# Hybrid SSD/S5 block on one core: the gate stage's x reaches token-major form by block transposes and transfers, and ScalarE applies dt

## The reference, cut to what matters

```
cb     = einsum("bclgn,bcsgn->bgcls", Cc, Bc)          # per group: tokens x tokens
decay  = exp(segsum(A))                                 # per head: tokens x tokens, lower triangle
y_diag = einsum("bgcls,bgrcls,bcsgrp->bclgrp", cb, decay, x * dt)
y      = (y_diag + d_skip * x) * silu(z), then an RMS norm over each group's 384 channels
```

## Time and profile before

| what | value |
|---|---|
| median of the runs | 1680.54 us (1680.04 to 1681.38) |
| the profiled execution's own time | 1680.3 us |
| its span, first to last instruction | 1678.6 us |
| PE busy | 1667.1 us (99%) |
| DVE busy | 1320.3 us (79%) |
| ACT busy | 962.7 us (57%) |
| POOL busy | 216.4 us (13%) |
| granted TensorE clock, mean | 0.998 of full |
| DMA, mean | 214 GB/s |

### The profile page before, as it was taken

One profiled execution on the slowest core, in us unless ns is written; L12 is line 12 of the kernel. 1 busy time (PEld: TensorE's weight loads), 2 busy tenths in 40 slices (PEclk: granted clock), 3 DMA queues, 4 the chain that ended last, 5 costly groups with the idle time before them and its releaser, 6 DMA issues.

```text
span 1678.6 us, 24422 instructions
## 1 busy us (share of the span) xinstructions
PE 1667.1 (99%) x8340; PEld 1395.1 (83%) x8340; DVE 1320.3 (79%) x1685; ACT 962.7 (57%) x1271; POOL 216.4 (13%) x310
## 2 busy tenths in 40 slices
PE   9999999999999999999999999999999999999997
PEld 8888888888788888888888888888888888888886
DVE  7999999999998986545775868888878888845555
ACT  7676676766666667444557755444444444454553
POOL 7843342221000000000000200000000000000001
PEclk9999999999999999999999999999999999999999
DMA  7666766666666566656786577777777777666653
GB/s 254 213 197 199 204 206 200 193 188 190 194 217 231 191 219 189 199 191 201 239 254 232 174 233 241 243 241 244 242 244 241 245 232 248 225 194 195 191 189 123
DMA packets 174569, 358.49 MB, mean 214 GB/s; under 512 B 16880, under 2 KB 39584, under 8 KB 174368
## 3 DMA queue, kind: packets, MB, share of 16 engines
q1 hardware_dynamic: 162528, 338.26, 62.5%
q0 software_dynamic: 11248, 18.37, 4.6%
q10 hardware_dynamic: 720, 0.93, 0.2%
HBM read 335.41 MB, written 15.80 MB: 209 GB/s over the span
## 4 chain that ended last, share of the span: by engine, by line
PE 73%; DVE 2%; issue 0%; ACT 0%; DVEq 0%
PE psum L1822 22%; PE psum L1823 22%; PE psum L1824 22%; PE psum L1783 3%; PE psum L1785 2%; PE psum L1908 1%; DVE wlo L1107 0%; PE psum L1909 0%; DVE vn L1749 0%; PE psum L1933 0%; DVE bc L1303 0%; PE psum L1829 0%; PE psum L1924 0%; DVE dec L1416 0%; PE psum L1982 0%; PE psum L1979 0%
## 5 line engine op out<-in xcount | busy, mean ns | idle before, releaser
L1107 DVE TENSOR_TENSOR wlo<-raw,whi 128x1024 fp32r<-128x1024 f32 x580 | 709.6, 1230 | 321.3 <-ACT whi L666 314.0
L666 ACT ACTIVATE whi<-raw 128x1024 fp32r<-128x1024 f32 x580 | 611.9, 1058 | 577.1 <-PE psum L1824 455.1
L1783 PE MATMUL psum<-act,whi 128*128 128x512 f32 x1088 | 342.5, 396 | 0.0
L1822 PE MATMUL psum<-whi,nw 128*128 128x512 f32 x704 | 274.1, 389 | 0.0
L1824 PE MATMUL psum<-whi,nw 128*128 128x512 f32 x704 | 273.9, 389 | 0.0
L1823 PE MATMUL psum<-wlo,nw 128*128 128x512 f32 x704 | 273.9, 389 | 0.0
L1785 PEld LDWEIGHTS psum<-act,wlo 128*128 128x128 f32 x1088 | 204.4, 188 | 48.3
L1785 PE MATMUL psum<-act,wlo 128*128 128x256 f32 x1088 | 213.7, 278 | 0.0
L1783 PEld LDWEIGHTS psum<-act,whi 128*128 128x128 f32 x1088 | 165.6, 189 | 3.3 <-issue 2.8
L1824 PEld LDWEIGHTS psum<-whi,nw 128*128 128x128 f32 x704 | 132.1, 188 | 27.6
L1822 PEld LDWEIGHTS psum<-whi,nw 128*128 128x128 f32 x704 | 132.1, 188 | 27.3
(11 more groups left out here) (251 smaller groups left out, 2300.3 us busy)
## 6 DMA issues: line engine op xcount, KB each, us to landing
raw<-in_w_up SPq DMA_DIRECT2D x176, 512.0 KB, 4.9
raw<-in_w_zx SPq DMA_DIRECT2D x96, 512.0 KB, 3.7
raw<-in_w_down SPq DMA_DIRECT2D x88, 512.0 KB, 3.8
raw<-in_w_gate SPq DMA_DIRECT2D x64, 512.0 KB, 5.6
raw<-in_w_proj SPq DMA_DIRECT2D x48, 512.0 KB, 4.4
raw<-in_w_bc SPq DMA_DIRECT2D x32, 512.0 KB, 3.7
raw<-in_w_glu SPq DMA_DIRECT2D x32, 512.0 KB, 4.4
raw<-in_w_out SPq DMA_DIRECT2D x32, 512.0 KB, 4.8
```

The lines of the kernel that those rows point to most:

```text
L666: fn(whi[:, s, :], raw[:, s, :], ACTF.Copy).then_inc(hi_ready, 1)
L1107: V.tensor_tensor(wlo[:, s, :], raw[:, s, :], whi[:, s, :], ALU.subtract).then_inc(lo_ready, 1)
L1783: mm(psum[:, b + t, :], whi[:, s, cols(t)], x, start=first, stop=False)
L1822: mm(banks[:, t, :], x_hi, high[:, k], start=j == 0 and k == 0, stop=False)
```

## The change

TensorE's six transposes a turn, ScalarE's copies to `bst` and `xst` and VectorE's two multiplications by dt go. In their place, for each group:

1. VectorE turns x in blocks of 32x32 (`x_turned`, two STREAM_TRANSPOSE instructions of 128x384): group 0's before the first bc turn, group 1's in turn 0 behind lo(4), group i+1's in turn i ahead of lo(2).
2. Four DMAs write the blocks to a scratch in DRAM (`token_write`, 96 KB each), and one DMA reads them back with tokens on the partitions into `xraw` (`token_fetch`, 384 KB). For group 0 SP issues these in the bc stage; for the others GpSimd does, around its decay loads.
3. ScalarE multiplies by dt (`tokens(g, k)`): 12 activations of 128x64 a turn, each with its own per-partition factor. They stand between hi(1) and decay(1), in turn 0 behind decay(1).

CB now reads B and C straight from `bc`; `heads(0)` waits for `xtok_ready` too. In turn 0 the transposes of dt move ahead of CB, and VectorE copies dt first.

The diff, cut to what the prediction speaks of:

```diff
@@ SP, bc stage @@
+                        if j == 6:
+                            first_tokens_write()
+                        if j == 24:
+                            first_tokens_fetch()
...
@@ GpSimd @@
-            with pool.Fori(0, GROUPS - 1) as i:
-                for half in range(2):
-                    pool.wait_ge(y_ready, i * 2 + (half + 1))
-                    load_decay(i + 1, half)
+            def token_write(g):
+
+                pool.wait_ge(x_blocks, g + 1)
+                for a in range(4):
+                    pool.dma_start(tokens_at[g % 2, :, :, a, :].rearrange("q j x -> j q x"),
+                                   xblk[g][32 * a:32 * a + 32, :, :, :, :].rearrange("j q k t i -> j q (k t i)")
+                                   ).then_inc(x_written, 16)
+
+            def token_fetch(g):
+
+                pool.wait_ge(x_written, 64 * g)
+                if g > 1:
+                    pool.wait_ge(xtok_ready, g)
+                pool.dma_start(xraw[g][:, :, :, :, :].rearrange("p a k t i -> p (a k t i)"),
+                               tokens_at[g % 2].rearrange("q j a x -> (q j) (a x)")).then_inc(x_read, 16)
+
+            for i in range(GROUPS - 1):
+                token_write(i + 1)
+                pool.wait_ge(y_ready, i * 2 + 1)
+                load_decay(i + 1, 0)
+                token_fetch(i + 1)
+                pool.wait_ge(y_ready, i * 2 + 2)
+                load_decay(i + 1, 1)
...
@@ ScalarE, gate_turn @@
-                def stage(g):
-                    fn(bst[:, :], bc[:, ds(g, 1), 0, :].rearrange("p o n -> p (o n)"), ACTF.Copy).then_inc(staged, 1)
-                    fn(xst[:, :, :], zx[:, ds(g * TPG, TPG), 1, :], ACTF.Copy).then_inc(staged, 1)
+                def tokens(g, k):
+
+                    act.wait_ge(x_read if g else first_read, 16 * max(g, 1))
+                    for hd in range(HPG):
+                        a = hd % 2 * 2
+                        ins = fn(xtok[:, k, 64 * hd:64 * hd + 64].rearrange("p (a i) -> p a i", a=2),
+                                 xraw[g][:, a:a + 2, k, hd // 2, :], ACTF.Identity,
+                                 scale=dtt[:, k, g * HPG + hd:g * HPG + hd + 1])
+                    if k == 1:
+                        ins.then_inc(xtok_ready, 1)
...
                     decay(1)
+                    act.wait_ge(dtt_ready, 1)
+                    tokens(0, 0)
+                    tokens(0, 1)
                 else:
                     hi(0)
                     decay(0)
                     hi(1)
+                    tokens(i, 0)
+                    tokens(i, 1)
                     decay(1)
...
-                if not last:
-                    act.wait_ge(cb_ready, i + 1)
-                    act.wait_ge(xp_ready, i + 1)
-                    stage(i + 1)
...
@@ VectorE @@
+            def x_turned(g):
...
+                for k in range(2):
+                    ins = V.transpose(xblk[g][:, :, k, :, :].rearrange("p q t i -> p t q i"),
+                                      zx[:, TPG * g:TPG * g + TPG, 1, k * P:k * P + P]
+                                      .rearrange("p t (q i) -> p t q i", q=4))
+                ins.then_inc(x_blocks, 1)
+
+            x_turned(0)
             mixer_turn("bc", 0, 6, ("zx", 5, 3))
...
-                    for k in range(2):
-                        ins = V.tensor_tensor(
-                            xtok[:, k, :].rearrange("p (h n) -> p h n", h=HPG),
-                            XP[k].rearrange("p (h n) -> p h n", h=HPG),
-                            dtt[:, k, ds(i * HPG, HPG)].rearrange("p (h o) -> p h o", o=1).to_broadcast([P, HPG, 64]),
-                            ALU.mult)
...
                     if not first_scan:
                         lo(1)
+                    if i < GROUPS - 1:
+                        x_turned(i + 1)
                     lo(2)
...
                 lo(4)
+                if prev is None:
+                    x_turned(1)
                 lo(5)
...
@@ TensorE, gate_turn @@
                     pe.wait_ge(m_ready, i * 2 + (half + 1))
+                    if half == 0:
+                        pe.wait_ge(xtok_ready, i + 1)
...
-                for k in range(2):
-                    for t in range(TPG):
-                        ins = nc.tensor.transpose(XP[k][:, t * P:t * P + P], xst[:, t, k * P:k * P + P], ident[:, :])
-                ins.then_inc(xp_ready, 1)
```

More of the change, by code:

```diff
@@ L164, in build_program @@
         dec = [at(f"dec{k}", [P, HALF, ML], F32, W + k * 4608) for k in range(2)]
-        xst = at("xst", [P, TPG, L], F32, W + 9216)
+        xblk = [at(f"xblk{g}", [P, 4, 2, TPG, 32], F32, off * K)
+                for g, off in enumerate((154, 140, 140, 140, 152, 152, 152, 152))]
+        xraw = [at(f"xraw{g}", [P, 4, 2, TPG, 32], F32, off)
+                for g, off in enumerate((147 * K, *[W + 9216] * (GROUPS - 1)))]
         xtok = at("xtok", [P, 2, HPG * 64], F32, W + 12288)
@@ L335, in up_fetch, with first_tokens_write, first_tokens_fetch @@
                              blocks_at.rearrange("j p q x -> (j p) (q x)")).then_inc(up_read, 16)
+            def first_tokens_write():
+                sp.wait_ge(x_blocks, 1)
+                for a in range(4):
+                    sp.dma_start(tokens_at[0, :, :, a, :].rearrange("q j x -> j q x"),
+                                 xblk[0][32 * a:32 * a + 32, :, :, :, :].rearrange("j q k t i -> j q (k t i)")
+                                 ).then_inc(first_written, 16)
+            def first_tokens_fetch():
+                sp.wait_ge(first_written, 64)
+                sp.wait_ge(cz_ready, 16)
+                sp.dma_start(xraw[0][:, :, :, :, :].rearrange("p a k t i -> p (a k t i)"),
+                             tokens_at[0].rearrange("q j a x -> (q j) (a x)")).then_inc(first_read, 16)
             for c in range(4):
@@ L353, in _ @@
                     sp.dma_start(craw[:, :, :, :], a["s5_c"]).then_inc(c_in, 16)
+                if name == "bc":
+                    for j in range(groups * quads):
+                        n = UNIT0[name] + j
+                        sp.wait_ge(lo_ready, n - RING + 1)
+                        sp.dma_start(raw[:, n % RING, :], a["w_bc"][j]).then_inc(w_in[n % RING], 16)
+                        if j == 6:
+                            first_tokens_write()
+                        if j == 24:
+                            first_tokens_fetch()
+                    continue
                 if name == "up":
@@ L770, in group_tap @@
                 act.nop(nofuse=True)
+                if name == "bc" and i == 0 and r == 1:
+                    act.wait_ge(first_written, 64)
                 for t in range(2):
@@ L864, in gate_turn @@
                     act.wait_ge(y5_ready, 8)
-                    act.wait_ge(xbc_done, 16)
-                    stage(0)
                     group_tap("bc", 1, 3)
@@ L898, in gate_turn @@
                 act.wait_ge(unit_used, u0 + 8)
+                if i == GROUPS - 2:
+                    act.wait_ge(x_written, 64 * (GROUPS - 1))
                 fn(gates[:, i, :, :], chunk_banks("gate", i), ACTF.Copy).then_inc(gate_free, 1)
@@ L1390, in _ @@
                 step.leave(6)
+            def x_turned(g):
+                if g == 0:
+                    dve.wait_ge(xbc_done, 2)
+                elif g == 1:
+                    dve.wait_ge(y5_ready, 8)
+                elif g == GROUPS - 1:
+                    dve.wait_ge(xbc_done, 12)
+                if g > 1:
+                    dve.wait_ge(x_written, 64 * (g - 1))
+                for k in range(2):
[4 more added lines that the diff above has]
+            x_turned(0)
             mixer_turn("bc", 0, 6, ("zx", 5, 3))
@@ L1424, in blocks, with mask_cb @@
                                     ALU.mult).then_inc(m_ready, 1)
-                def tokens():
+                def mask_cb():
                     dve.wait_ge(cb_ready, i + 1)
-                    V.tensor_tensor(cbm[:, :], CB, mask_in[:, :], ALU.mult)
-                    dve.wait_ge(xp_ready, i + 1)
                     if prev is None:
-                        step.done(V.tensor_copy(dtt[:, :, :], DTT))
-                    for k in range(2):
-                        ins = V.tensor_tensor(
-                            xtok[:, k, :].rearrange("p (h n) -> p h n", h=HPG),
-                            XP[k].rearrange("p (h n) -> p h n", h=HPG),
-                            dtt[:, k, ds(i * HPG, HPG)].rearrange("p (h o) -> p h o", o=1).to_broadcast([P, HPG, 64]),
-                            ALU.mult)
-                    step.done(ins)
+                        V.tensor_copy(dtt[:, :, :], DTT).then_inc(dtt_ready, 1)
+                    step.done(V.tensor_tensor(cbm[:, :], CB, mask_in[:, :], ALU.mult))
                 if prev is None:
@@ L1449, in gate_turn @@
                     lo(3)
-                    tokens()
+                    mask_cb()
                     blocks(0)
@@ L1921, in gate_turn @@
                     pe.wait_ge(y5_out, 8)
```

(8 more changed lines are left out.)

10 lines of the change are left out of this document (6 added, 4 removed).

## The result

The changed kernel takes 1683.03 us (median of 14 runs, 1681.72 to 1686.47), the kernel before 1680.53 (14 runs on the same chip, 1679.68 to 1681.65): a ratio of 1.0015, 95% interval 1.0008 to 1.0022. It is slower by 2.5 us, or 0.15%, where 1680.2 was forecast, 0.3 us faster. The profiled execution spans 1680.9 us instead of 1678.6.

The account below looks back on a forecast made before the run. TensorE's list of matmuls bounds the kernel. Turn 1's unit 6 starts 3.5 us later, turns 2 to 7 give back 6 x 0.58 = 3.5, sum 0.0: 1680.3 us, forecast as 1680.2, range 1676.4 to 1684.0.

Parts of the forecast that it names:

- TensorE's 0.58 a turn: Gate stage: dropping TensorE's six transposes saves 0.58 us a turn, in turns 1 to 7, 4.1 us if nothing becomes late.
- the two delays that were named: Turn 1: twelve activations, 2.9 us, delay decay(1); group 1's decay loads issue behind transposes and writes, near 462.6 and 466.7.
- A: Rival: decay(1) of turn 1 starts at most 0.7 us later, so 4.1 us come off, 1676.2 us; chance 0.16.
- C: Rival: ScalarE's small activations cost 0.38 us a start, 4.6 a turn; 4.6 us lost in all, 1684.9; chance 0.08.
- D: Rival: TensorE's time between CB and the next unit stays, nothing comes back in turns 2 to 7, 1683.8; chance 0.07.
- Turn 1, summed: Turn 1: decay(1) starts 4.1 us later; less 0.68 slack, TensorE's unit 6 starts 3.5 us later than now.
- the load chain: GpSimd, turn 0: writes land at 466.1, then the fetch; the second decay load, issued at 466.7, lands at 473.6.
- waits at units 5 and 6: Sign in the profile: TensorE waits for `wlo` at units 5 and 6 of turn 1, 3 us or more together.
- rival B: Group 1's second decay load lands late behind write, wait and read, deciding from 477.9 on; 4.9 us, 1685.2; chance 0.11.
- The forecast's lower end: With activations at 0.16 us a start, decay(1) of turn 1 at 475.3, sum -1.9 us: 1678.4 us.
- I take no cost: Turns 2 to 7: decay loads 1 to 4 us later and 0.75 MB more a turn were priced at nothing.
- the ring of four weights: Turns 2 to 7: a weight unit that lands late has the ring of four ahead of it, so no cost.

Follow-up runs that it names:

- e6: Changed kernel with both group-1 decay loads ahead of GpSimd's writes in turn 0 and 11 of ScalarE's 12 activations of turn 1 left out; 1679.92 us.
- e9: e6 with 11 of ScalarE's 12 activations left out in turns 2 to 7 too, all transfers kept; 1678.27 us.
- e4: Changed kernel with six 128x128 transposes put back on TensorE behind the C B products in each of turns 2 to 7; 1685.90 us.
- e13: e12 with 14 more 128x512 matmuls on TensorE between units 4 and 5 of turn 1; 1681.20 us.
- e12: Changed kernel with 11 of ScalarE's 12 activations left out in turns 2 to 7, turn 1 as in the changed kernel; 1682.56 us.
- e10: e6 with the scratch writes and fetches of x in turns 2 to 7 cut to 32 bytes a row, activations kept; 1678.62 us.
- e8: Kernel before, with only group 1's second decay load held until TensorE is done with unit 2 of turn 1; 1685.59 us.
- e2: Changed kernel with 11 of ScalarE's 12 activations of turn 1 left out, GpSimd's order as in the changed kernel; 1682.47 us.
- e5: Changed kernel with both group-1 decay loads ahead of GpSimd's writes and fetch in turn 0, run once for its profile rows; 1680.39 us.

## Why the prediction was wrong

*What held.* TensorE's 0.58 a turn was 0.63. Turn 0 gave nothing: the wait grew to 1.35. VectorE's pair took 1.03, the twelve activations 2.96, and lo(4) did wait for ScalarE. Turn 1 was the place of the loss, with the two delays that were named, the twelve ahead of decay(1) and the queue on GpSimd; rivals A, C and D fell (A: e6 and e9 show the gain coming through only with turn 1 mended; C: the activations took 0.25 us a start; D: e4).

*The step that failed* is "Turn 1, summed", where unit 6 was to start 3.5 us later; it started 5.7 later. Two terms were off. The smaller is the load chain: writes landed at 467.48 instead of 466.1, the load was issued at 468.31 instead of 466.7, so scan(1) and not the activations set decay(1), at 477.35 instead of 477.1. Unit 6's `wlo` was done at 482.92 + 1.22 = 484.14, 3.7 behind the 480.44 of before; that part was 0.2 off. The larger was not in the sum at all: the prediction asked when `wlo` is ready, and took TensorE's own work between the stop and unit 6 as it was. But the 3.44 us of idle time were followed by half the clock, unit 5 took from 478.48 to near 483.9, and unit 6 started 486.10 - 484.14 = 2.0 behind its `wlo`. Putting matmuls into the idle time takes this away, in e13 against e12, at 1.36 us in the medians. The prediction did list waits at units 5 and 6, "3 us or more together", among its signs, but neither its sum nor any of its rivals has a price for what follows the first.

This is also not rival B. B's mechanism (the second load behind a write, a landing and a fetch) did bind and stopped unit 5, but by its own threshold, a landing at 477.9, it did not decide: the load landed at 474.63.

That 1683.03 lies within the range given (1676.4 to 1684.0) is luck. The upper part of that range, 1683.1, was worked out for landings of 9.8 us, and the one that counted took 6.33. The forecast's lower end has a slip of its own: at 0.16 a start decay(1) was put at 475.3, but by the same paragraphs scan(1) ends only at 476.2, which makes about 1679.4 of its 1678.4. The miss does not hang on it.

*The second failure* is the sentence "I take no cost" for the later loads and the added bytes in turns 2 to 7, with the ring of four weights as cover. The ring covers a late weight on TensorE's side but not on ScalarE's, where 2.96 us stand in front of the root. e9 and e10 show that it takes both, for 1.3 to 1.65 us in e6's kernel. In the changed kernel it cost 0.26 us in turn 6 of the profiled run; the 0.5 in the median is within the spread.

*The sum as measured,* from the profiled spans: 5.7 lost by unit 6 of turn 1, 3.9 back from there to the start of the proj stage, which leaves 1.7 (643.68 against 641.94); 0.4 more in the proj stage's first units, and 0.2 at the end: 2.3. The forecast's 3.5 lost and 3.5 back was right in kind.

## What to carry to other kernels

Where a change makes an engine that sets the time wait, price not only the wait but the speed of what comes behind it: for TensorE, read the granted clock of that stretch, not only the busy share. A transfer that needs a wait of its own on an issuing engine belongs behind every transfer that is already due there. When two delays lie over each other, undoing either one alone shows little (1.2 and 0.6 of 3.1 us here); undo both before calling either harmless.

## What the hardware showed that was not expected

TensorE's granted clock fell to 0.50 behind idle times of 3.44 us (the changed kernel), 3.6 (e8), 3.8 (e12) and 4.1 (e2), and to 0.62 in the mean of the stretch behind 2.7 us (e5). In e4 it fell too, but only some 1 us after the end of 4.33 us of idle time (0.70 in the mean of the stretch from 479.1 to 482). Behind e6's 1.7 us it stayed at 1.00, as it did where matmuls filled the idle time (e13). In the kernel before, TensorE's one stop in the gate stage was 0.76 us. The Trainium skill, "TensorE: Matmul & The Clock Gate", Part 1 on the clock gate, says that an idle array drops to the lower of its two clocks; the 0.50 above agrees, and what it costs here is e13's 1.36 us, or the 0.8 to 2.3 us of the profiles.
